# Cached keys turned by VectorE during the FFNs and kept in HBM, and a scan that adds the positive part of the scores itself

## What is computed

```
def decoder_layer(x, past_k, past_v, s0, buf, past_len, p):
    x = half_ffn(x, ..., p['ffn1_w_gate'], p['ffn1_w_up'], p['ffn1_w_down'])
    m, k_new, v_new, s_new, buf_new = mixer(rms_norm(x, p['mix_norm_pre']), past_k, past_v, s0, buf, past_len, p)
    x = x + rms_norm(m, p['mix_norm_post'])
    x = half_ffn(x, ..., p['ffn2_w_gate'], p['ffn2_w_up'], p['ffn2_w_down'])
```

```
z = jnp.einsum('bqhd,bkhd->bhqk', qblk, kf) * scale + bf
log_1mb = jnp.where(mask, jax.nn.log_sigmoid(-z), 0.0)
tail = lax.cumsum(log_1mb, axis=3, reverse=True) - log_1mb
w = jnp.where(mask, jnp.exp(jax.nn.log_sigmoid(z) + tail), 0.0)
out = jnp.einsum('bhqk,bkhd->bqhd', w, vf)
```

## Time and profile before

| | us |
|---|---|
| median of 3 runs | 1406.8 |
| profiled execution: span, first to last instruction | 1407.3 |
| TensorE busy (matmul) | 1391.1 |
| VectorE busy | 899.6 |
| ScalarE busy | 734.5 |
| GpSimd busy | 182.6 |
| mean granted TensorE clock, share of full | 0.998 |

### The profile page before, as it was taken

The page is one execution under the profiler, slowest core; times in us unless marked ns, Lnnn a source line. Parts: engine busy times, 40 slices in busy tenths (PEclk is TensorE's granted clock), DMA queues, the critical chain, the costliest instruction groups (busy, mean ns, idle before and its releaser), DMA issues.

```text
span 1407.3 us, 26950 instructions
## 1 busy us (share of the span) xinstructions
PE 1391.1 (99%) x10551; PEld 1321.4 (94%) x10551; DVE 899.6 (64%) x1508; ACT 734.5 (52%) x1210; POOL 182.6 (13%) x333
## 2 busy tenths in 40 slices
PE   7999999999999999999999999999999999999998
PEld 6999999988878999999999999999888799999998
DVE  5666544669995876663367665346899858756542
ACT  4544434489766554443365444346887665444441
POOL 1020000323262110000000000021433510000000
PEclk9999999999999999999999999999999999999999
DMA  9575455577799595545545555564868895555541
GB/s 247 150 210 150 141 147 153 156 203 230 210 310 265 145 255 150 150 139 152 155 127 149 151 149 144 152 175 141 252 206 242 287 255 154 151 149 149 148 139 50
DMA packets 391554, 249.41 MB, mean 177 GB/s; under 512 B 16513, under 2 KB 379638, under 8 KB 391428
## 3 DMA queue, kind: packets, MB, share of 16 engines
q1 hardware_dynamic: 375602, 204.94, 51.2%
q0 software_dynamic: 15520, 42.62, 9.7%
q10 hardware_dynamic: 306, 0.13, 0.0%
HBM read 242.10 MB, written 5.53 MB: 176 GB/s over the span
## 4 chain that ended last, share of the span: by engine, by line
PE 94%; DVE 2%; ACT 1%; DMA 1%; issue 1%; SPq 0%; POOLq 0%; POOL 0%; DVEq 0%; ACTq 0%
PE bank L596 25%; PE bank L598 24%; PE bank L597 24%; PE bank L862 3%; PE bank L973 2%; PE bank L877 2%; PE bank L632 2%; PE bank L636 2%; PE bank L633 2%; PE bank L1050 1%; DMA raw<-in_ffn_w_gate 1%; PE bank L827 1%; PE bank L954 1%; PE bank L1168 1%; PE bank L1090 1%
## 5 line engine op out<-in xcount | busy, mean ns | idle before, releaser
L1602 DVE TENSOR_TENSOR w_l<-raw,w_h 128x1024 fp32r<-128x1024 f32 (+1 forms) x332 | 395.4, 1196 | 295.4 <-ACT w_h L1224 295.1
L596 PE MATMUL bank<-hh,w_h 128*128 128x320 f32 x1632 | 512.9, 314 | 0.0
L598 PE MATMUL bank<-hh,w_l 128*128 128x320 f32 x1632 | 504.4, 309 | 0.0
L597 PE MATMUL bank<-hl,w_h 128*128 128x320 f32 x1632 | 504.3, 309 | 0.0
L1224 ACT ACTIVATE w_h<-raw 128x1024 fp32r<-128x1024 f32 (+1 forms) x332 | 332.3, 1030 | 141.4 <-DMA raw<-in_ffn_w_down 101.4
L596 PEld LDWEIGHTS bank<-hh,w_h 128*128 128x128 f32 x1632 | 306.4, 188 | 11.8 <-issue 8.6
L597 PEld LDWEIGHTS bank<-hl,w_h 128*128 128x128 f32 x1632 | 306.5, 188 | 0.6
L598 PEld LDWEIGHTS bank<-hh,w_l 128*128 128x128 f32 x1632 | 306.4, 188 | 0.0
L596 PE MATMUL bank<-guh,w_h 128*128 128x320 f32 x704 | 217.7, 309 | 0.0
L598 PE MATMUL bank<-guh,w_l 128*128 128x320 f32 x704 | 217.4, 309 | 0.0
L597 PE MATMUL bank<-gul,w_h 128*128 128x320 f32 x704 | 217.4, 309 | 0.0
(11 more groups left out here) (297 smaller groups left out, 1604.9 us busy)
## 6 DMA issues: line engine op xcount, KB each, us to landing
raw<-in_ffn_w_gate SPq DMA_DIRECT2D x88, 512.0 KB, 4.0
raw<-in_ffn_w_up SPq DMA_DIRECT2D x88, 512.0 KB, 3.9
raw<-in_ffn_w_down SPq DMA_DIRECT2D x64, 448.0 KB, 3.8
raw<-in_w_in SPq DMA_DIRECT2D x44, 512.0 KB, 4.0
raw<-in_ffn_w_down SPq DMA_DIRECT2D x32, 512.0 KB, 4.0
kpg<-in_cache_sb_k SPq DMA_DIRECT2D x112, 128.0 KB, 3.3
kpg<-in_cache_sb_k POOLq DMA_DIRECT2D x112, 128.0 KB, 2.7
raw<-in_w_out SPq DMA_DIRECT2D x16, 512.0 KB, 6.9
```

The source lines that it names most:

```text
L596: pe.matmul(out, w_h[:, slot, k, :], rhs_h[:, k0 + k, :], start=first, stop=False)
L597: pe.matmul(out, w_h[:, slot, k, :], rhs_l[:, k0 + k, :], start=False, stop=False)
L598: last = pe.matmul(out, w_l[:, slot, k, :], rhs_h[:, k0 + k, :], start=False, stop=end)
L1602: V(dve.tensor_tensor(w_l[:, slot, 0:n, :], raw[:, slot, 0:n, :], w_h[:, slot, 0:n, :].bitcast(F32), ALU.subtract), sm["w_lo"])
```

## The change

The transposes of cached keys on TensorE, ScalarE's copies of them, `kpz` and `kpg` go. In their place the keys of a layer are turned before its mixer, during FFNs, in 32 units of one sequence x 4 pages (512 KB). For each unit GpSimd issues 4 loads, one for each page, into 32 partitions of `kn_` each (4 rows of 1 KB to a partition); VectorE transposes 32x32 blocks of 128x1024 elements from `kn_` to `kx_` in one instruction; GpSimd issues 4 stores from 32 partitions each to a new HBM tensor `turned_keys` (256 runs of 512 B each). `kn_` and `kx_` have two buffers. Layer 0's 32 units are all turned in the first FFN (one after each pair of gate step 1 to 10, two after each down step 0 to 5); layer 1's 16 + 16 in the second and third (one in each step). In the mixer the turned keys come back in one load of 4 KB per partition for each sequence and round, into `kT`, 8 rounds instead of 16 halves; a round's scores are 8 products of 512 columns, and their bank alternates. ScalarE makes max(z,0) as a third activation (`zp`), and VectorE's scan takes `zp` and `t_` as its two tensors with add, add. A few start-up semaphores are merged: the first transposes wait for `const` with `x_loaded0`, TensorE's first mean for `const`, `level` and `pages` together.

```
-TURNS = {7: (0,), 8: (1,), 9: (2,), 10: (3, 4), 11: (5,), 12: (6, 7), 13: (8,), ...
-KEYS_EARLY = ((0,), (0, 1))
+SCORES_AT = {9: 0, 10: 1, 12: 2, 13: 3, 15: 4, 17: 5, 19: 6, 21: 7}
+SCORE_BANK = (4, 2)
...
+    turned_keys = nc.dram_tensor("turned_keys", [L, ITS, G, P, 2, 4, P], F32, kind="Internal").ap()
...
 SyncE (b in (0, 1)); GpSimd the same for b in (2, 3)
-                def keys(h):
+                def keys(it):
+                        if it < 2:
+                            sp_.wait_ge(sm["w_used"], U + U_IN + 4)
                         else:
-                            sp_.wait_ge(*at("kt_turned", 4 * (h - 2) + b + 1))
-                        for j in range(2):
-                            sp_.dma_start(heads(kpg[l][:, h % 2, b, j, :]), page(sp_, ids[4 * b + 2 * (h % 2) + j], ins["cache_sb_k"], l)).then_inc(sm[f"ks_loaded{h % 2}"], 16)
+                            sp_.wait_ge(*at("kt_used", it - 1))
+                        sp_.wait_ge(sm[f"kx_stored{b}"], 64 * (l * UNITS_K // 2 + 2 * it + 1))
+                        sp_.dma_start(kT[l][it % 2][:, b], turned_keys[l, it, b].rearrange("p a n s -> p a (n s)")).then_inc(sm[f"ks_loaded{it % 2}"], 16)
...
 GpSimd
+                def load_rows(i):
+                    g = l * UNITS_K + i
+                    if g >= 2:
+                        pool.wait_ge(sm["kx_turned"], g - 1)
+                    page_ids(pool, ids, i // G, (i % G,))
+                    for n in range(4):
+                        pool.dma_start(kn_[32 * n:32 * n + 32, g % 2], quarter(pool, ids[n], ins["cache_sb_k"], l)).then_inc(sm[f"kn_loaded{g % 2}"], 16)
+                def store_turned(i):
+                    g = l * UNITS_K + i
+                    pool.wait_ge(sm["kx_turned"], g + 1)
+                    for n in range(4):
+                        pool.dma_start(turned_keys[l, i // G, i % G, :, :, n, :].rearrange("(r p) a s -> p a r s", p=32),
+                                       kx_[32 * n:32 * n + 32, g % 2].rearrange("p (a r) s -> p a r s", a=2)).then_inc(sm[f"kx_stored{g % 2}"], 16)
...
                 if l:
                     pool.wait_ge(sm["v_used"], l * per["v_used"])
+                    pool.wait_ge(so, 80 * l)
+                    pool.wait_ge(sm["conv_out"], 48 * l)
                 else:
-                    pool.wait_ge(sm["w_used"], 16)
+                    pool.wait_ge(sm["w_used"], 8)
-                for h in range(2):
-                    for b in range(G):
-                        for j in range(2):
-                            pool.dma_start(heads(kpz[:, h, b, j, :]), page(pool, ids[4 * b + 2 * h + j], ins["cache_sb_k"], l)).then_inc(sm["kz_loaded"], 16)
+                load_rows(0)
+                load_rows(1)
+                for i in range(UNITS_K):
+                    store_turned(i)
+                    if i + 2 < UNITS_K:
+                        load_rows(i + 2)
+                all_stored(pool, l)
                 pool.wait_ge(sm["w_used"], U + U_IN)
...
 ScalarE, place_scores
                     else:
                         act.wait_ge(*at("lw_ready", it))
+                    A(nsa(zp[:, :], bank[SCORE_BANK[it % 2]][:, :], ACT.Relu, bias=bq[:, :]))
...
 VectorE
+            def turn_keys(k2, units):
+                for _ in range(units):
+                    if staged[0] >= (1, 1.5, 2, 2)[k2] * UNITS_K:
+                        return
+                    g = staged[0]
+                    dve.wait_ge(sm[f"kn_loaded{g % 2}"], 64 * (g // 2 + 1))
+                    if g >= 2:
+                        dve.wait_ge(sm[f"kx_stored{g % 2}"], 64 * (g // 2))
+                    V(dve.transpose(kx_[:, g % 2].rearrange("p c (j s) -> p j c s", s=32), kn_[:, g % 2].rearrange("p j (c d) -> p j c d", d=32)), sm["kx_turned"])
+                    staged[0] += 1
...
+                        if i and (k2 == 0 or t == 0):
+                            turn_keys(k2, 1)
...
+                    if n < KD - 2:
+                        turn_keys(k2, 2 if k2 == 0 else 1)
...
-                    V(dve.scalar_tensor_tensor(t_[:, :], z, 0.0, t_[:, :], ALU.max, ALU.add))
-                    V(dve.tensor_tensor_scan(s[:, ::-1], cst_("ones", cols=1).to_broadcast([P, 512]), t_[:, ::-1], later, ALU.mult, ALU.add))
+                    V(dve.tensor_tensor_scan(s_[:, ::-1], zp[:, ::-1], t_[:, ::-1], later, ALU.add, ALU.add))
```

More of the change, by code:

```diff
@@ L303, in build @@
     assert a[0] >= end_ffn and gul_at + 11 * T * 4 <= st_at and st_end <= gul_end
-    kpz = sb("kpz", [P, 2, G, 2, 256], at=[a[0]])
+    k_at = [end_ffn]
+    kn_ = sb("kn_", [P, 2, 4, 256], at=k_at)
+    kx_ = sb("kx_", [P, 2, 8, P], at=k_at)
+    assert k_at[0] <= nc.sbuf_usable_end
     wT = sb("wT", [P, ITS, 4, P], at=[a[0]])
@@ L359, in page, with quarter, all_stored @@
         return cache[l:l + 1, bass.ds(eng.snap(reg, min_val=0, max_val=cache.shape[1] - 1), 1)].rearrange("l n p h d -> p (l n h) d")
+    def quarter(eng, reg, cache, l):
+        return cache[l:l + 1, bass.ds(eng.snap(reg, min_val=0, max_val=cache.shape[1] - 1), 1)].rearrange("l n (j p) h d -> p (l n j) (h d)", p=32)
+    def all_stored(eng, l):
+        for half in range(2):
+            eng.wait_ge(sm[f"kx_stored{half}"], 64 * (l + 1) * UNITS_K // 2)
     def heads(ap):
@@ L446, in _ @@
                     load_in(m + 3)
-                    for h in range(4, 2 * ITS):
-                        if SLOT_OF[h - 2] == m:
-                            keys(h)
+                    for it in range(2, ITS):
+                        if SCORED[it - 2] == m:
+                            keys(it)
                 for it in range(ITS):
@@ L876, in scores @@
                             c0 = (it // (PAGES // 4) * G + b) * 32
-                            last = pe.matmul(bank[4][32 * b:32 * b + 32, h % 2 * 256:(h % 2 + 1) * 256],
-                                             qb[:, p_, c0:c0 + 32], kpz[:, h, b, p_, :] if h in KEYS_EARLY[l] else kT[l][:, h % 2, b, p_, :],
+                            last = pe.matmul(out[32 * b:32 * b + 32, :], qb[:, p_, c0:c0 + 32], kT[l][it % 2][:, b, p_, :],
                                              start=(p_ == 0), stop=(p_ == 1), skip_group_check=True)
@@ L1013, in _ @@
                         gate_rows(u, out, range(4))
-                    elif h == last_h:
+                    else:
                         unit(u, out, hh, hl, part=range(4))
-                    else:
-                        unit(u, out, hh, hl, part=range(3))
-                        turn_keys(h, (2, 3))
-                        unit(u, out, hh, hl, part=range(3, 5))
-                        turn_keys(last_h, (0, 1))
-                        unit(u, out, hh, hl, part=range(5, 6))
-                        scores(h)
-                        unit(u, out, hh, hl, part=range(6, 7))
-                    if last_h < 2 * ITS:
-                        turn_keys(last_h, (2, 3))
                     if m == 9:
@@ L1044, in _ @@
                     else:
-                        unit(u, out, hh, hl, part=range(4, KD) if h == last_h else range(7, KD))
+                        unit(u, out, hh, hl, part=range(4, KD))
                 def gla_outputs(pair):
@@ L1926, in _ @@
                         place_prompt(m - 13)
-                    for h in TURNS[m]:
-                        if h >= 2 and h % 2 == 0:
-                            log_weights(h // 2 - 1)
+                    if m in SCORES_AT:
+                        log_weights(SCORES_AT[m])
                     if m == NIN - 1:
```

214 lines of the change are left out of this document (70 added, 144 removed).

## The result

| kernel | median of the runs, us | range of the runs | ratio to before, 95% interval |
|---|---|---|---|
| before | 1407.4 | 1406.1 to 1408.7 | |
| changed | 1416.8 | 1412.5 to 1419.4 | 1.0063 [1.0043, 1.0083] |

The change makes the kernel 0.6% slower, where 1397 us and "faster" were forecast. The profiled execution of the changed kernel (span 1410.9 us) is the one of 1412.5 us, the shortest of the four: a time is 1.6 us longer than the span of the same execution, and 4.3 us of the median stand in no trace.

A forecast was written before the change was run, and what follows sets the result against it. TensorE, busy 99% of the span, was taken as the bound, with VectorE slowest in the mixers after the change. 1407.3 - 5.2 - 26 + 21 = 1397.1 us, forecast 1397; 8 times in 10 from 1366 to 1442.

The forecast's parts named there:

- The first FFN: All 32 units of layer 0 must load, turn and store there: cost taken as 21 us, bounds 0 and 91.
- by bytes: First FFN: 64.2 MB of keys and weights at 290 GB/s need 221 us, 21 us too much.
- The loop term: First FFN: issue, landing and turn with two units in flight, 6.6 us each, need 213 us, 13 too much.
- Rival B: First FFN: key transfers in pieces of 32 partitions move slower; 1427 us at 1.6 times the price; chance 0.33.
- The early transposes: 48 transposes between blocks, with nothing else on TensorE's path: 5.2 us, all gained.
- The mixers: Both mixers: transposes leave TensorE, VectorE becomes slowest, half of its waits go; 13 us gained in each, 26 together.
- The scan's part: Layer 0's mixer: VectorE loses 8 additions of max(z,0), 5.5 us; the scan's second real tensor costs nothing.
- the scores: Mixers: a round becomes one set of 8 products of twice the width; 0 to 16 us possible, 0 taken.
- the reloads: Mixers: loading turned keys back, the same 2.1 MB per round, costs 0; without cover a few us per layer.
- the turn: FFNs: VectorE's transpose of one unit takes 1.2 us; 32 are 39 us where VectorE idles about 90.

## Why the prediction was wrong, by its steps

**The first FFN (+21 forecast; +24.8 measured, +25.1 against the run with layer 0 unturned).** This is the step that failed. The prediction took the larger of its two workings, "by bytes" at 290 GB/s, and came within 4 us of the size by luck, since neither working is what happened. The kernel moved 283 GB/s, and the 227 us from 48 to 275 make 64 MB of it, as worked out. But 283 was no limit of the bytes: as many went at 311 GB/s with the loads spread and at 315 with a third buffer, and without the stores the rate fell to 226. Nor was 290 GB/s the rate of a full DMA. It is the mean of 22 us of which the first 4 moved 125 GB/s, and its key loads all land in 128 partitions. Beside the 336 GB/s from 488 to 500 us stand these two stretches of the kernel before, with the same columns:

```profile
484.00:488.00 4.00, 4.00 (x29) 4.00 (x28) 3.95 (x7) 0.00 (x0) 1.81 (x2) 1.00 0.42 125
...
500.00:506.00 6.00, 6.00 (x43) 6.00 (x42) 4.20 (x7) 3.20 (x5) 0.00 (x0) 1.00 1.13 310
```

What set the rate is where the loads land: side by side in 32 partitions they make the weights land after 14.3 us and the FFN end at 280.4, spread over the range the same bytes end it at 262.1. The loop term (13 us) was no better. The turns stand 6.7 us apart in the first gate steps, near the 6.6 worked out, but they do so with wide loads and a third buffer too: there is one turn in each pair, and VectorE's pairs, 5.6 us apart in the same place before, are 6.7 with it. With narrow loads a third buffer didn't help; with wide ones it gave 4.4 us of this FFN (262.5 to 258.1).

**Rival B** named the right cause, pieces of 32 partitions slower than those of 128, and had 0.33. Its price was too high, its stores cost nothing, and its mark (an end beyond 285 us, waits for keys from the first gate steps on) did not come: the end was at 280, and 41.6 us of the waits came after 180 us, 3.3 before. The forecast chose between B and the bytes, where B's cause was what set the rate of the bytes.

**The early transposes (-5.2)**: 0.3 us gained in the first FFN (layer 0 unturned), nothing in the second and third. "Nothing else on TensorE's path" was read from a chain in which they stood; that chain has 0.7 us of wait for `hh` right behind, which the view of TensorE's waits would have shown.

**The mixers (-26)**: -12.9 and -9.2, inside the bounds of 7.4 to 18.5 each. The mechanism is as forecast, with VectorE at 97.5%. TensorE's waits in the second one, 960 to 1162 us:

```profile
PE bank L831 <- DVE gk L1806: 4.8, 1, 4.8
PE bank L846 <- DVE att L1785: 2.2, 2, 2.0
PE bank L957 <- DMA vpg1b<-in_cache_sb_v: 2.2, 1, 2.2
```

The first two are in mixer 0 too (4.8 and 2.0); the wait for values is 0.3 before. Over the runs with both parts of the change the mixers lie at 199.2 to 204.0, a gain of some 11 us each. The term is 4 us oversized. From entry to end VectorE's busy time fell by 6.4 us in mixer 0 (168.3 to 162.0) and 5.8 in mixer 1 (168.1 to 162.4), and its idle time by 6.6 and 3.5. So the half of the waits that was taken as gained came in mixer 0 and not in mixer 1. What holds mixer 1 back beyond the 2 us for values was not tried, and neither was what TensorE's lower granted clock costs (0.97 over mixer 0 and 0.98 over mixer 1, 1.00 and 0.99 before).

**The scan's part, the scores, the reloads, the turn**: costed at 5.5 us of VectorE's time in each mixer, 0, 0 and 1.2 us. The first is 5.3 us of the total over both mixers, the set of scores is twice the old one for half the sets, no wait for a reload stands among TensorE's waits of mixer 1, and the turn is 1.24.

**The sum**: 5.6 + 4.3 + 3.9 + 0.1 = 13.9 us from 1397.1 give the profiled 1410.9 (0.1 by rounding). The 5.6 are 4.1 of the turns' cost and 1.5 of the early transposes. To the median it is 5.9 more, which no term had: 1.6 from the span to the time of the same execution, and 4.3 since the other executions were 3.4 to 6.9 us longer than the profiled one. Their mean granted clock was lower, 0.978 to 0.980 against 0.983; what lengthened them stays open, since they left no trace.

**The range** held the time (1366 to 1442); the chance of "slower" was 0.37, under the 0.55 of "faster". No single term turned a gain of 10 us into a loss of 9: they all fell short, the first FFN by the most, and there the mechanism was wrong too.

## What to carry to other kernels

When a change adds transfers beside a stream that feeds the slowest engine, ask first in which partitions they land: 32 side by side cost 20 us here (1416.8 against 1396.5), and 32 spread over the range, a change of one slice, gave it back. (The keys then lie in another order and would have to be read by it, as they are in the run with loads over 128 partitions.) A DMA share of 1.1 does not mean that bytes are the limit: compare GB/s at that share in two stretches before taking one as the rate. Work that is taken from the slowest engine is only a gain if that engine doesn't wait at the same place, and a part that is worth nothing alone can be worth 5 us with the other.

## What the runs showed of the hardware that was not expected

- Loads into neighbouring partitions slow the other queue's transfers too: the weights' packets, whose shape is unchanged, took 4.5 to 5.3 us of all 16 DMA engines for a MB, against 3.6 beside spread loads, and in the changed kernel landed after 14.3 us against 6.0.
- Stores from 32 neighbouring partitions cost no time against stores from 128 (1416.8 and 1414.6; 1395.7 and 1396.1 us): only the writing side into the on-chip memory was sensitive.
- GpSimd's time to issue a store of 256 runs of 512 B was 613 ns from 32 partitions and 853 to 890 from 128. Halved to 128 runs, from 128 partitions, it was still 697: 8 such stores cost 5.6 us where 4 of twice the size cost 3.4 to 3.6.
- Fewer bytes can be slower to finish than more: 45 MB with narrow loads ended the first FFN at 267.8 us, 62 MB with wide ones at 262.5.
